# Eight places for the value tiles of the sample attention, and the prompt half of the first output job ahead of the samples' transposes

## What is computed

```python
def cross_attend(h, k, v, g_pre, w_q, w_o, g_post):
    n = rms_norm(h, g_pre)
    q = (n @ w_q).reshape(bsz, L, X_HEADS, X_HEAD_DIM)            # 4 heads x 256
    s = jnp.einsum('blhd,bmhd->bhlm', q, k).astype(jnp.float32) * (X_HEAD_DIM ** -0.5)
    p = jax.nn.softmax(s, axis=-1).astype(v.dtype)
    o = jnp.einsum('bhlm,bmhd->blhd', p, v).reshape(bsz, L, X_HEADS * X_HEAD_DIM)
    return h + rms_norm(o @ w_o, g_post)
```

## Time and profile before

| | us |
|---|---|
| three runs | 1720.32, 1721.32, 1721.12 |
| median | 1721.12 |
| profiled execution, its own time | 1720.17 |
| its span | 1718.4 |
| PE busy | 1612.5 (94%) |
| DVE busy | 1040.2 (61%) |
| ACT busy | 671.0 (39%) |

### The profile page before, as it was taken

How to read it: one execution, slowest core, us unless ns; L and a number is a source line. 1 busy time by engine, 2 the same in 40 slices (tenths; PEclk the granted TensorE clock), 3 DMA queues, 4 the chain that set the end, 5 groups by cost and what they waited for, 6 DMA issues and landing times.

```text
span 1718.4 us, 28425 instructions
## 1 busy us (share of the span) xinstructions
PE 1612.5 (94%) x11770; PEld 1555.7 (91%) x11770; DVE 1040.2 (61%) x1426; ACT 671.0 (39%) x1084; POOL 203.8 (12%) x179
## 2 busy tenths in 40 slices
PE   7899999999999979997989989789999999999997
PEld 6899999999999969996879749689999999999996
DVE  4773674575377467999444432686357547646744
ACT  5451453354155343221543333445235325424531
POOL 2020220121021000004010010002012012102200
PEclk9999999999999989998989999899999999999997
DMA  4232322233233222223233541122323223322321
GB/s 144 74 98 74 91 87 94 78 96 98 75 99 100 97 82 74 99 76 105 98 116 135 173 170 50 50 74 75 98 75 99 99 73 94 105 74 75 99 75 55
DMA packets 137904, 159.16 MB, mean 93 GB/s; under 512 B 3198, under 2 KB 130770, under 8 KB 137769
## 3 DMA queue, kind: packets, MB, share of 16 engines
q1 hardware_dynamic: 131648, 136.06, 24.9%
q0 software_dynamic: 6032, 21.19, 3.5%
q10 hardware_dynamic: 96, 0.02, 0.0%
HBM read 152.22 MB, written 5.40 MB: 92 GB/s over the span
## 4 chain that ended last, share of the span: by engine, by line
PE 80%; DVE 14%; ACT 3%; issue 1%; DMA 1%; POOL 0%; ACTq 0%; DVEq 0%; POOLq 0%
PE slot L1708 38%; PE slot L1832 36%; DVE f L1530 6%; DVE wp L1162 2%; PE slot L1752 1%; ACT wp L664 1%; DVE f L1198 1%; PE slot L1766 1%; PE slot L2055 1%; PE slot L2074 1%; DVE h L1202 1%; DVE f L1242 1%; DVE folded L1177 1%; DMA kring<-in_cache_mem_v_dram 0%; PE slot L1736 0%
## 5 line engine op out<-in xcount | busy, mean ns | idle before, releaser
L1832 PE MATMUL slot<-nb,wu 128*128 128x288 f32 x4704 | 632.8, 295 | 11.0 <-issue 6.3
L1832 PEld LDWEIGHTS slot<-nb,wu 128*128 128x128 f32 x4704 | 628.4, 188 | 13.2 <-issue 8.5
L1708 PE MATMUL slot<-mid,wp 128*128 128x288 f32 x4224 | 580.2, 298 | 28.6 <-DVE wp L1162 15.1
L1708 PEld LDWEIGHTS slot<-mid,wp 128*128 128x128 f32 x4224 | 570.9, 191 | 35.0 <-issue 25.9
L664 ACT ACTIVATE wp<-raw 128x1024 fp32r<-128x1024 f32 x120 | 127.0, 1058 | 388.1 <-PE slot L1708 371.3
L1162 DVE TENSOR_TENSOR wp<-raw,wp 128x1024 fp32r<-128x1024 f32 x120 | 147.0, 1225 | 130.4 <-ACT wp L664 130.4
L581 POOL TENSOR_TENSOR raw<-raw,q 128x512 f32<-128x512 f32 x56 | 80.3, 1433 | 865.6 <-DVE wu L1298 553.0
L1708 PE MATMUL slot<-n,wp 128*128 128x288 f32 x1152 | 167.9, 307 | 13.1 <-DVE n L1184 10.8
L1708 PEld LDWEIGHTS slot<-n,wp 128*128 128x128 f32 x1152 | 162.1, 197 | 17.8 <-issue 13.6
L1426 DVE TENSOR_TENSOR f<-slot,f 128x576 f32<-128x576 f32 x48 | 36.3, 756 | 134.6 <-PE slot L1708 134.6
L1530 DVE SCALAR_TENSOR_TENSOR f<-glu,convw,f 128x512 f32<-128x512 f32 x240 | 111.7, 543 | 0.0
(11 more groups left out here) (236 smaller groups left out, 1383.1 us busy)
## 6 DMA issues: line engine op xcount, KB each, us to landing
raw<-in_ffn_w_gate_dram SPq DMA_DIRECT2D x32, 1024.0 KB, 5.4
raw<-in_ffn_w_up_dram SPq DMA_DIRECT2D x32, 1024.0 KB, 5.4
raw<-in_ffn_w_down_dram SPq DMA_DIRECT2D x32, 1024.0 KB, 4.9
raw<-in_mix_w_in_dram SPq DMA_DIRECT2D x8, 1024.0 KB, 5.1
kring<-in_cache_mem_k_dram POOLq DMA_DIRECT2D x6, 1024.0 KB, 5.4
kring<-in_cache_mem_v_dram POOLq DMA_DIRECT2D x6, 1024.0 KB, 5.6
raw<-in_xattn_w_k_dram SPq DMA_DIRECT2D x4, 1024.0 KB, 4.9
raw<-in_xattn_w_v_dram SPq DMA_DIRECT2D x4, 1024.0 KB, 4.9
```

The lines of the kernel that those rows point to most:

```text
L1708: ins = pe.matmul(slot(u)[:, half, 0:HALF], wp[:, J % 2, wi, kt], X(xi, kt, half), start=kt == 0 and k == 0, stop=kt == KT - 1 and k == le ...
L1832: ins = pe.matmul(dst[:, 0:HALF], wu[:, p, wi, kt], nb[:, p, xi, kt], start=start and kt == 0 and k == 0, stop=kt == KH - 1 and k == len(P ...
```

## The change

Each value tile of the samples has a place of its own. Tile 5 lies over `kT` (a further view `v5` of `region_w`) and is issued third, once `sc3` has been computed. Tiles 6 and 7 lie in the two halves of `raw`, viewed as value tiles, and are issued by SP, at the places in its queue where output slabs 1 and 2 stood. Slab 1 is loaded when PE has used tile 6 (`vs_used` 7), slab 2 when PE has filled `pvs`. PE does `pt3` before `ss7`. The first output job is written out in two passes: its 24 matmuls of columns 0 to 287, then the transposes of the samples' result (`turn_samples`), then its 24 matmuls of columns 288 to 575. The other seven jobs are as before.

```diff
@@ the plan
-    pl.use("ss7", "pt3", "pv0", "pv1", "pv2", "sprob", *[f"pv{o}" for o in range(3, 8)], "pvs", "pvt")
+    pl.use("pt3", "ss7", "pv0", "pv1", "pv2", "sprob", *[f"pv{o}" for o in range(3, 8)], "pvs", "pvt")
@@ region_w
+                   [("wpv", [P, 2, PARTS, KT, P], PDT), ("v5", [P, MT, D], F32)])
@@ places and semaphores
+        o_slab = pl.base["o"][0] // 2
+        values = [kring[:, 0], kring[:, 1], kring[:, 2], vx[:, 0], vx[:, 1], v5[:, :, :]] + [
+            raw[:, s % RAW].rearrange("p k c -> p (k c)").rearrange("p (t d) -> p t d", t=MT) for s in (o_slab + 1, o_slab)]
+        values_in = [(ld_v[i], 16) for i in range(6)] + [(ld_x[i], 32) for i in range(2)]
@@ SP
-            load_static("glu0", 28)
+            load_static("glu0", 25)
+            sp.wait_ge(wlo, prepared(2 * (o_slab - 1)) + 2)
+            sp.dma_start(values[6], cv[6].rearrange("(t p) d -> p t d", p=P)).then_inc(values_in[6][0], 16)
+            sp.wait_ge(wlo, prepared(2 * o_slab) + 2)
+            sp.dma_start(values[7], cv[7].rearrange("(t p) d -> p t d", p=P)).then_inc(values_in[7][0], 16)
+            sp.wait_ge(vs_used, 7)
+            sp.dma_start(raw[:, (o_slab + 1) % RAW], static_slab(o_slab + 1)).then_inc(loaded[(o_slab + 1) % RAW], 16)
+            wait_aux(sp, "pvs")
+            sp.dma_start(raw[:, (o_slab + 2) % RAW], static_slab(o_slab + 2)).then_inc(loaded[(o_slab + 2) % RAW], 16)
+            load_slab(o_slab + 3, static_slab(o_slab + 3))
             load_ffn("ffn2")
@@ POOL
-            for b in range(NB):
+            for b in (0, 1, 5, 2, 3, 4):
                 if b < 3:
                     wait_aux(pool, f"ktb{4 + b}")
-                elif b < 5:
+                elif b == 5:
+                    wait_aux(pool, "sc3")
+                else:
                     wait_aux(pool, f"ss{3 + b}")
@@
-                else:
-                    pool.wait_ge(vs_used, b - 5 + 1)
-                dst = vx[:, b - 3] if 3 <= b < 5 else kring[:, b % 5]
-                pool.dma_start(dst, cv[b].rearrange("(t p) d -> p t d", p=P)).then_inc(ld_v[b % 5], 16)
+                pool.dma_start(values[b], cv[b].rearrange("(t p) d -> p t d", p=P)).then_inc(values_in[b][0], 16)
@@ PE
-            sample_scores(7)
             turn_probs(3)
+            sample_scores(7)
@@
-                pe.wait_ge(ld_v[b % 5], 16 * (b // 5 + 1))
-                vals = vx[:, b - 3] if 3 <= b < 5 else kring[:, b % 5]
+                pe.wait_ge(*values_in[b])
+                vals = values[b]
@@
-            jobs("o", half_of(mid), attended)
+            J, u = start_job("o", 0)
+            for half in range(2):
+                for kt in range(KT):
+                    if half == 0:
+                        wait_freed(pe, f"pv{kt}")
+                    elif kt == 0:
+                        turn_samples()
+                        wait_freed(pe, "pvt")
+                    for k, (wi, xi) in enumerate(PRODUCTS):
+                        ins = pe.matmul(slot(u)[:, half, 0:HALF], wp[:, J % 2, wi, kt], mid[:, xi, kt, half * HALF:(half + 1) * HALF],
+                                        start=kt == 0 and k == 0, stop=kt == KT - 1 and k == len(PRODUCTS) - 1)
+            ins.then_inc(job_done, 1)
+            for i in range(1, KT):
+                job("o", i, half_of(mid))
```

More of the change, by code:

```diff
@@ L204, in build @@
                    [("wu", [P, 7, PARTS, KH, P], PDT), ("q13", [P, 2, KH, P], F32)],
-                   [("wp_", [P, 2, PARTS, KT, P], PDT), ("b12", [P, PARTS, KH, HALF], PDT)])
+                   [("wp_", [P, 2, PARTS, KT, P], PDT), ("b12", [P, PARTS, KH, HALF], PDT)],
+                   [("wpv", [P, 2, PARTS, KT, P], PDT), ("v5", [P, MT, D], F32)])
         R, acc, part = (rr[k] for k in ("R", "acc", "part"))
-        wp, kT, vtok, wu, q13, b12 = (rw[k] for k in ("wp", "kT", "vtok", "wu", "q13", "b12"))
+        wp, kT, vtok, wu, q13, b12, v5 = (rw[k] for k in ("wp", "kT", "vtok", "wu", "q13", "b12", "v5"))
         above = PARTS * KT * T
@@ L273, in build @@
         ld_k = [sem(f"ld_k{i}") for i in range(4)]
-        ld_v = [sem(f"ld_v{i}") for i in range(5)]
+        ld_v = [sem(f"ld_v{i}") for i in range(6)]
         id_set, const_set, masked, bd_zero, glu_zero, eps_set = (
@@ L2066, in _ @@
                     turn_probs(i - 1)
+            turn_probs(3)
             sample_scores(7)
-            turn_probs(3)
             def head_out(o):
@@ L2097, in _, with turn_samples @@
                 ins.then_inc(vs_used if b < NB - 1 else filled, 1)
[L2098 to L2106, removed]
-            jobs("o", half_of(mid), attended)
+            def turn_samples():
+                pe.wait_ge(os_ready, 1)
+                wait_freed(pe, "pvs")
+                turn("pvt", [(aux("pvt")[:, 0, (2 * g + d) * P:(2 * g + d + 1) * P], os_[:, g, d * P:(d + 1) * P])
+                             for g in range(2) for d in range(2)])
+            J, u = start_job("o", 0)
[12 more added lines that the diff above has]
+                job("o", i, half_of(mid))
             sum_squares("post3")
```

## The result

The changed kernel takes 1708.45 us, the median of four runs (1706.83 to 1710.02), against 1720.77 for the kernel before; the ratio is 0.9926, 95% interval 0.9911 to 0.9942. It is faster, by 12.3 us where 10.85 were forecast. The forecast was 1710.3, with a range of 1708.4 to 1713.6. The measured median lies at its lower end. The profiled execution is the fastest of the four, 1706.83 us.

A forecast was written before the change was run, and what follows sets the result against it. PE, busy 94%, was taken to bound the kernel, with late value-tile loads costing waits and slow matmuls. Gains of 6.55 + 1.0 + 3.3 = 10.85 us from the median 1721.12 gave 1710.3 us, range 1708.4 to 1713.6.

The forecast's parts named there:

- What bounds the kernel: PE is busy 94%; around the sample value tiles late `kring` loads cost waits and half-speed matmuls behind them.
- Part 1: Sample value tiles all loaded ahead: 13.66 to about 7.1 us, gain 6.55 (4.13 idle, 2.4 half-speed matmuls); late slabs cost 0.
- Part 2: `pt3` ahead of `ss7` at the end of the scores: scores fill PE's 1.31 us wait for `pT`, gain 1.0 us.
- Part 3: Prompt half of output job 0 first: value tiles' end to job's end 8.45 us against 11.8, gain 3.3.
- the 2.8 us that I booked to it: Clock staying at full speed behind the value tiles: 0.5 us in the transposes, 2.3 in output job 0's matmuls.
- The sum: Whole kernel: 6.55 + 1.0 + 3.3 = 10.85 us gained.
- The sign that came: Prediction wrong if the stretch from job 0's end to program's end is not as long as before within 1 us.
- A: Rival: the clock falls in the 1.63 us wait left in output job 0, costing 1.7 to 2.1 us; 1712.2; chance 0.12.
- B: Rival: softmax, tiling switch or slab 1 cover too thin, or clock rises later in the norm; 1711.5 to 1714; chance 0.10.
- C: Rival: slower than before because output slab 1 lands late and delays job 2; 1725 with 28 us; chance 0.02.
- D: Rival: waits remain because tile 6 or 7 waits for a place in `raw`; gain some 2 us, 1719; chance 0.02.

The follow-up runs named there:

- null_before: The kernel before, run once more with no edit; 1719.57 us, ratio 0.9994 beside 23 runs of the same kernel.
- slab_late: The changed kernel with output slab 1 issued only when output job 0 is done, about 9.7 us later; 1713.12 us in one run.
- values_only: The kernel before with only the eight places for the value tiles, old `pt3` order and job 0 in one piece; 1714.02 us, ratio 0.9958; second profile 1715.16 us.
- the two repeats: The changed kernel, run twice more with no edit; 1710.46 us (ratio 0.9941) and 1709.11 us (ratio 0.9937) against the kernel before.
- swap_only: The kernel before with only `pt3` put ahead of `ss7`; 1720.62 us, ratio 1.0002.
- half_only: The kernel before with only the prompt half of output job 0 put ahead of the transposes of the samples' result; 1719.35 us, ratio 0.9995.

## Why the prediction was right or wrong

**What bounds the kernel, right.** The waits for the loads into `kring` and the slow matmuls behind them were the cost, and the changed profile has neither.

**Part 1, right in size.** 6.55 us were put down for the value tiles; 13.66 and 13.54 us went to 7.11 and 7.12. Of the 2.4 that I put down as half-speed matmuls about 0.6 belong to something else: tile 5 of null_before, standing alone between two waits, takes 1.07 us at full speed, and 0.87 in a run of tiles. That the late slabs 1 and 2 cost nothing was right, and slab_late shows from where on they do.

**Part 2, right.** 1.0 was forecast, 1.1 measured with the change and with the swap alone. The bare switch from 32-column to 128-column matmuls, which I had bounded by 0.13 us, cannot be seen: the value tiles' row ends at 1021.76 by the model, and the job's begins at 1021.69. The Trainium skill (TensorEngine Tiling (Array Packing), Key Properties) has the engine drain at a change of tiling mode; this trace shows no idle time for it.

**Part 3, right in the sum.** 3.3 forecast; 3.06 beside null_before (56.60 to 53.54), where the jobs take 6.40 us in both. Two things in it were off. The end of job 0 comes 8.9 us behind the value tiles and not 8.45. Of this, 0.17 is that a matmul takes 0.1335 us and not 0.130; most of the rest is that the two pieces of job 0 end in a pause (3.43 and 3.48 us by PE's rows, where 24 x 0.1335 is 3.20), which a plain 24 x 0.130 leaves out. And values_only shows that the clock is not the merit of the places: of the 2.8 us that I booked to it, they bring 0.9. The prompt half ahead brings 2.2 more (55.71 to 53.54), 0.6 of them the hidden wait.

**The sum, right within 1 us.** 10.85 forecast; 9.5 to 10.6 us by the traces of the stages, 11.0 by the means of all runs, 10.1 and 10.7 by the medians of the two repeats.

**What failed: the base and the range.** The step was "the median of the runs is 1721.12, 0.95 above that execution, so I forecast 1710.3", with a lower end only 1.9 us below. It took three runs within 1 us, and one profile, for the kernel's own constancy. With all runs the 1.85 us between forecast and result fall into three parts: the base is 1720.5 and not 1721.1 (0.6), the gain is 11.4 by medians and not 10.85 (0.5), and the four runs of the result lie 0.7 below the median of all 15. 66 runs spread from 1712.3 to 1724.9, four of the changed kernel from 1706.8 to 1710.0, so a median of four is itself uncertain by about 1 us, and the profile's stages by more: ahead 5.2 us, rest 3.5, norm 1.1, output jobs 1.2. The lower end reached for particular mechanisms (a better norm, 1.5 us, which did not come: 44.38 in both first profiles), and left out the plain scatter. A range of 3.5 us either way would have said what was known. I also took the 6.23 us of an output job for its length at full speed. Of 14 profiles that one alone had it there, and the 6.40 of the q jobs, in the same trace and at the same granted clock, could have warned me.

**The sign that came.** The prediction called itself wrong if the stretch from the end of job 0 to the end of the program was not as long as before to within 1 us. It was 2.0 us shorter in the first pair: 3.1 shorter behind the output jobs, 1.1 longer within them. The repeats show both as differences that unchanged code has too, so the sign was narrower than the kernel's own scatter and does not speak against the mechanism.

**The rivals.** A did not come, in three profiles of the changed kernel; its argument from a wait of 1.8 us at 467.5 pointed the right way, but its quantity, the longest idle time alone, does not decide it. B appeared in none of its forms. C and D fell as argued: the slab was not waited for, and both value tiles in `raw` were issued by 957.69.

## What to carry to other kernels

Here a late load cost its wait and the clock of the matmuls behind it, so places for all tiles of a short burst were worth more than the sum of the waits (6.55 us against 4.13); but with two waits close behind the burst the clock was lost there instead, in both profiles of values_only. How much a fall of the clock costs changes from one execution to the next, so one profile does not price it. Work that needs only half of an operand's columns can be put ahead of the chain that makes the other half, for as many jobs as have their weights and PSUM ready. And before a gain of half a per cent is explained by the trace, profile the same code twice: compare stage by stage, and leave out every stage that differs as much between two profiles of one kernel.

## What the runs showed that I had not expected

Jobs of the same 48 matmuls at clock 1.00 take 6.23 us in one stretch and 6.40 in another, mostly through a whole projection (52.12 against 53.37 us for 384 matmuls with a slow start), and 13 of 14 profiles hold both. What sets the one or the other stays open. No run was made for it.

The clock's fall does not follow the longest idle time: kept behind 2.68 us in dense work, lost behind 3.61 there, lost behind 2.16 among value tiles, lost twice behind 0.59 and 1.63 with 0.6 us between them. And it can rise inside a stretch of waits: in swap_only it was up again before job 0 began, which alone moved that execution by 2 us. half_only was as lucky, so its trace says little of what the prompt half is worth with late value tiles.
